# Loading weight tiles in pairs: one 2 MB transfer and one signal for two tiles

## What is computed

```
def reference(x, mem, ...):
    x = first_block(x, mem, ...)
    return second_block(x, c_2, ...)

first_block:
    proj = rmsnorm(h) @ w_in                    # conv, q, k, v, q_mem and gate columns
    y_conv = conv_module(u_conv, ...) @ w_conv_out
    y_attn = chunk_attention(q, k, v, rel_bias) @ w_attn_out
    kv = rmsnorm(mem) @ w_mem_kv
    y_mem = memory_attention(qm, km, vm) @ w_mem_out
    h = h + (g0 * y_conv + g1 * y_attn + g2 * y_mem) @ w_o
    val, gt = split(causal_dwconv(rmsnorm(h) @ w_up))
    h = h + (silu(gt) * val) @ w_down
second_block:
    mod = silu(c) @ ada_w + ada_b               # six vectors of 2048
    x = x + g1 * token_mixer(h, w_in, ...)      # four kinds of attention
    x = x + g2 * moe_ffn(h, ...)                # 16 experts, each token uses two of one group of four
```

## Time and profile before

| | us |
|---|---|
| median of 3 runs | 3329.46 |
| their range | 3325.71 to 3338.23 |
| the profiled execution | 3333.14 |
| its span in the profile | 3331.4 |
| PE busy | 3166.1 (95%) |
| DVE busy | 2060.5 (62%) |
| ACT busy | 1420.9 (43%) |
| DMA, mean of the span | 208 GB/s |

### The profile page before, as it was taken

One profiled execution on the slowest core, in us unless ns is written; L12 is line 12 of the kernel. 1 busy time (PEld: TensorE's weight loads), 2 busy tenths in 40 slices (PEclk: granted clock), 3 DMA queues, 4 the chain that ended last, 5 costly groups with the idle time before them and its releaser, 6 DMA issues.

```text
span 3331.4 us, 54295 instructions
## 1 busy us (share of the span) xinstructions
PE 3166.1 (95%) x21868; PEld 2979.2 (89%) x21868; DVE 2060.5 (62%) x2409; ACT 1420.9 (43%) x1531; POOL 69.7 (2%) x171
## 2 busy tenths in 40 slices
PE   6899999998998999999999799999897999999997
PEld 6789699998998999999999799977696988989887
DVE  4434347887664889889888533124453586685774
ACT  4433353434434444444444332123332465475562
POOL 0000100000000000000000000002100000000000
PEclk8999699999998999999999898575596999999999
DMA  6335245553553788788887664222230688596782
GB/s 222 139 132 184 91 169 188 178 187 139 205 190 118 301 332 320 307 327 315 322 321 287 182 209 151 76 60 50 65 114 7 250 337 316 217 381 228 303 325 88
DMA packets 114005, 694.25 MB, mean 208 GB/s; under 512 B 13984, under 2 KB 27536, under 8 KB 32464
## 3 DMA queue, kind: packets, MB, share of 16 engines
q1 hardware_dynamic: 107648, 671.14, 53.8%
q10 hardware_dynamic: 4688, 13.11, 1.4%
q0 software_dynamic: 1536, 8.13, 0.9%
HBM read 681.83 MB, written 10.49 MB: 208 GB/s over the span
## 4 chain that ended last, share of the span: by engine, by line
PE 90%; DVE 5%; DMA 2%; ACT 1%; issue 1%; SPq 0%; DVEq 0%; ACTq 0%
PE psT L847 17%; PE psT L848 17%; PE psT L849 17%; PE psT L1198 2%; PE psT L1200 2%; PE psT L1199 2%; PE psY L968 2%; PE psT L1187 2%; PE psT L1189 2%; PE psT L1188 2%; PE psY L940 2%; PE psT L892 1%; PE psY L1005 1%; PE psT L893 1%; PE psT L894 1%; PE psY L1088 1%
## 5 line engine op out<-in xcount | busy, mean ns | idle before, releaser
L1312 DVE TENSOR_TENSOR w_lo<-raw,w_hi 128x2048 fp32r<-128x2048 f32 x532 | 1217.1, 2291 | 693.0 <-ACT w_hi L491 689.9
L491 ACT ACTIVATE w_hi<-raw 128x2048 fp32r<-128x2048 f32 x532 | 1016.7, 1912 | 661.1 <-PE psT L849 204.2
L847 PE MATMUL psT<-a_hi,w_hi 128*128 128x256 f32 x4304 | 1227.1, 285 | 53.2 <-DVE a_lo L1339 48.0
L848 PE MATMUL psT<-a_lo,w_hi 128*128 128x256 f32 x4304 | 1224.8, 285 | 0.0
L849 PE MATMUL psT<-a_hi,w_lo 128*128 128x256 f32 x4304 | 1224.5, 284 | 0.0
L847 PEld LDWEIGHTS psT<-a_hi,w_hi 128*128 128x128 f32 x4304 | 833.7, 194 | 55.6 <-issue 50.6
L848 PEld LDWEIGHTS psT<-a_lo,w_hi 128*128 128x128 f32 x4304 | 833.7, 194 | 0.1
L849 PEld LDWEIGHTS psT<-a_hi,w_lo 128*128 128x128 f32 x4304 | 833.4, 194 | 0.0
L1525 DVE CUSTOM_DVE_ANT_0 pool<-pool 128x2048 f32<-128x2048 f32 x96 | 219.3, 2284 | 0.0
L847 PE MATMUL psT<-h_hi,w_hi 128*128 128x256 f32 x704 | 200.7, 285 | 5.8 <-DVE h_lo L1557 5.7
L848 PE MATMUL psT<-h_lo,w_hi 128*128 128x256 f32 x704 | 200.4, 285 | 0.0
(11 more groups left out here) (275 smaller groups left out, 3868.3 us busy)
## 6 DMA issues: line engine op xcount, KB each, us to landing
raw<-tiles_dram SPq DMA_DIRECT2D x532, 1024.0 KB, 5.3
pool<-ada_tiles_dram SPq DMA_DIRECT2D x96, 1024.0 KB, 4.8
bias_rows_dram<-pool ACTq DMA_DIRECT2D x1, 8192.0 KB, 50.4
pool<-bias_rows_dram SPq DMA_DIRECT2D x40, 128.0 KB, 2.2
pool<-w_dram POOLq DMA_DIRECT2D x8, 512.0 KB, 6.3
pool<-bias_rows_dram SPq DMA_DIRECT2D x40, 64.0 KB, 1.8
pool<-mem_dram ACTq DMA_DIRECT2D x1, 2048.0 KB, 13.5
pool<-x_dram ACTq DMA_DIRECT2D x1, 2048.0 KB, 23.8
```

Source lines behind the costliest of these rows:

```text
L491: nc.scalar.activation(w_hi[:, t.k % SPL, :], raw[:, t.k % RAW, :], ACT.Copy).then_inc(hi_done, 1)
L847: nc.tensor.matmul(ps_out, wh, x_hi, start=first, stop=False)
L848: nc.tensor.matmul(ps_out, wh, x_lo, start=False, stop=False)
L1312: nc.vector.tensor_tensor(w_lo[:, t.k % SPL, :], raw[:, t.k % RAW, :], w_hi[:, t.k % SPL, :].bitcast(F32), ALU.subtract).then_inc(lo_done, 1)
```

## The change

Two tiles are loaded by one DMA into two neighbouring places of the ring, and there are two semaphores, one for each pair of places. `load_tile` does nothing for an odd tile. For an even tile t it waits for `lo_done` of tile t - 3, so that both places are free, and issues one transfer of 2 MB. The destination names 128 partitions, 2 tiles, 2048 elements. `load_expert` does the same in steps of two. `split` waits for the pair's semaphore, for either tile of the pair. The ring's size, the order on ACT, DVE and PE, and the ada loads are as before.

```diff
-        landed = [sem(f"tile_landed{s}") for s in range(RAW)]
+        landed = [sem(f"tiles_landed{s}") for s in range(RAW // 2)]
...
             def load_tile(t):
-                wait(sp, lo_done, (t + -RAW).count())
-                sp.dma_start(raw[:, t.k % RAW, :], tiles[t.k if t.i is None else t.i * t.n + t.k])\
-                    .then_inc(landed[t.k % RAW], 16)
+
+                if t.k % 2:
+                    return
+                wait(sp, lo_done, (t + (1 - RAW)).count())
+                at = t.k if t.i is None else t.i * t.n + t.k
+                sp.dma_start(raw[:, t.k % RAW:t.k % RAW + 2, :], tiles[bass.ds(at, 2)].rearrange("t p n -> p t n"))\
+                    .then_inc(landed[t.k % RAW // 2], 16)
...
-                for k in range(4):
+                for k in (0, 2):
                     t = Tile(at + k)
-                    wait(sp, lo_done, (t + -RAW).count())
-                    sp.dma_start(raw[:, t.k % RAW, :], tiles[group[s] * 48 + (BASE["moe"] + 12 * j + 4 * part + k)])\
-                        .then_inc(landed[t.k % RAW], 16)
+                    wait(sp, lo_done, (t + (1 - RAW)).count())
+                    first = group[s] * 48 + (BASE["moe"] + 12 * j + 4 * part + k)
+                    sp.dma_start(raw[:, t.k % RAW:t.k % RAW + 2, :], tiles[bass.ds(first, 2)].rearrange("t p n -> p t n"))\
+                        .then_inc(landed[t.k % RAW // 2], 16)
...
-                act.wait_ge(landed[t.k % RAW], t.plus(16 * (t.k // RAW + 1), 16 * (t.n // RAW)))
+                act.wait_ge(landed[t.k % RAW // 2], t.plus(16 * (t.k // RAW + 1), 16 * (t.n // RAW)))
```

## The result

| us | before | after |
|---|---|---|
| median of 4 runs | 3328.57 | 3448.98 |
| their range | 3325.71 to 3338.23 | 3444.68 to 3459.76 |
| the profiled execution | 3333.14 | 3447.05 |
| its span | 3331.4 | 3445.3 |

The changed kernel takes 1.0361 times as long (95% interval 1.0329 to 1.0394): 3.6% slower, 17 us more than the 3432 us forecast and inside its range.

What follows compares the result with a forecast made beforehand. TensorE was taken to bound the kernel, with loads hidden. Kernel start 2, feed-forward 24, experts' start 2.4 and window runs 74 added 102.4 us to 3333.1, giving a median of 3432 us (3.1% slower), range 3392 to 3480.

Steps and rivals of the forecast that it cites:

- The trip of a ring place: All stages: load, w_hi, w_lo, next load must fit four tiles of PE, 23.0 us, or 10.9 in window runs.
- Plain stages: Attention weights, gates, projections: the later landing, 8.2 us in all for an even tile, stays hidden; cost 0.
- Window runs: Three runs of 40 window-expert tiles: rounds of 14.0 us against PE's 10.9 lose 67 us, 74 with spacing.
- the 7 us added for spacing: Window runs: loaded tiles stand 2.75 us apart, not 2.48; half of up to 4.9 us a run was added.
- Feed-forward: Feed-forward stage: 22 us of drift less 2 for w_lo's lead over PE, plus 4 at the start: 24 us.
- The drift: Feed-forward: DVE's chain takes 71.3 us per 12 tiles against PE's 69.1, so 2.2 us too slow, ten groups.
- Start of the experts: Tile 340, which nothing hides, now lands with tile 341, 2.48 us later: cost 2.4 us.
- Kernel start: First tiles: the third tile lands with the fourth, so its w_lo ends at 32.2 instead of 30.2: cost 2 us.
- Rival 1: Whole kernel: lateness is hidden, same or slightly faster, 3322 us; needs 2 MB landing in under 4.2 us; chance 0.05.
- Rival 3: Window runs and feed-forward: a 2 MB load costs 0.5 us more than two of 1 MB, 3461 us; chance 0.15.
- Rival 2: Window runs: the clock also falls to 1.2 GHz in each of 27 rounds, 46 us more, 3480 us; chance 0.10.
- Granted clock 1.00 in the runs: Window runs: a sign expected in the profile after, the granted clock staying at its full value of 1.00.

Runs made afterwards that it cites:

- Plain pairs: Pair first's kernel with pairs kept only for tiles 0 to 339 and expert tiles loaded one by one: 3327.5 us, ratio to before 0.9958 to 1.0046.
- quads: Changed kernel taken one step further, four tiles in one 4 MB transfer into the whole ring with one signal: 4510.3 us in one run.
- Pair first: Changed kernel with each feed-forward pair load put ahead of the ada load it stood behind on SP: 3410.9 us.
- own signals: Changed kernel with pairs still issued together, but each tile having its own transfer and semaphore: 3357.4 us, ratio to before 1.0065 to 1.0138.
- late signal: Kernel before, with single loads issued as early, but w_hi of an even tile also waiting for the odd one: 3492.0 us.
- the two runs on shape: Changed kernel with each pair as two 1 MB transfers on one semaphore, 3442.4 us; or contiguous as 16 KB per partition, 3451.6 us.

## Why the prediction was right

**The method.** The trip of a ring place, compared with what PE needs for four tiles, named the two stages that lose and the ones that don't. Plain stages differ by -4.0 and -0.4 us. Plain pairs and quads show both sides of that limit. Of the 17 us between forecast and median, 11.5 lie in the stages. The other 5.6 lie between executions: the profiled execution before is now 4.6 us above its median (3.7 when the forecast was made), the one after 1.9 below. And the 11.5 are small partly by luck, since the clock took 4 us off in the plain stages.

**Window runs, 74 forecast, 86 measured.** The step held and its terms were small by little. With the 7 us added for spacing the forecast stood at 14.27 us a round; measured is 14.42. Landing took 7.5 us, not 7.3. The rounds make only 4 of the 12 us missing: nine of them, from the end of w_lo of tile 359 to that of tile 395 and so in the other two runs, took 128.8, 130.4 and 130.2 us against 128.4. Another 6 lie behind them, where the forecast had put nothing. PE starts on the last tile of a run 0.7, 0.7 and 2.0 us after its w_lo, and in two runs it then needs 1.7 and 1.3 us more for the next tile, whose w_lo ends 1.3 and 1.0 us after PE is done with the last. Some 1 us more comes from following the first run alone: in the kernel before, PE reached the last tile 103.8 us after the first w_lo there, but 103.1 in the other two. The Trainium skill (SBUF — State Buffer, The DMA setup-cost knee) would give 6.8 us for 2 MB, an estimate by its formula; measured is 7.5 to 7.6. For 4 MB the same estimate is 11.6, measured 12.3.

**Feed-forward, 24 forecast, 28 measured.** The drift was forecast at 2.2 us in 12 tiles. From tile 187 to 271, PE's distance to before at every twelfth tile is 5.4, 7.6, 9.9, 12.1, 14.1, 16.2, 18.4 and 20.6 us: 2.2 each. Its cause was the one named: rows of SP and DVE after the change, for tiles 202 and 203, the pair ahead of that of the earlier trace rows; the last row of SP is the pair twelve tiles on.

```profile
1354.81 0.33 SPq L429 DMA_DIRECT2D pool<-ada_tiles_dram  x1
1355.34 0.39 SPq L383 DMA_DIRECT2D raw<-tiles_dram  x1
...
1426.72 0.39 SPq L383 DMA_DIRECT2D raw<-tiles_dram  x1
```
```profile
1352.34 2.29 DVE L1530 CUSTOM_DVE_ANT_0 pool<-pool 128x2048 f32<-128x2048 f32 x1
...
1366.71 2.29 DVE L1317 TENSOR_TENSOR w_lo<-raw,w_hi 128x2048 fp32r<-128x2048 f32 x1 [0.29 <-ACT w_hi L496]
```

From the dot product's end (1354.63) to w_lo of the even tile (1366.71) are 12.1 us, as worked out. Tile 214, at the same place of the next twelve, is issued 71.4 us later (1355.34 to 1426.72), where 71.3 was worked out and PE needs 69.1. Pair first shows that it was this link. What was off were the ends. The start (tiles 152 to 167) cost 7.8 us where 4 was put and the last four tiles 2.6 us. The drift between them, to tile 279, came to 17.6 us, that of eight groups of twelve and not ten; I had put 22 and deducted 2 for the lead of w_lo.

**Start of the experts, 2.4 forecast, 3.9 measured.** I priced the pair's landing by the second of two single loads. SP and ACT after the change:

```profile
2603.20 0.96 SPq L473 DMA_DIRECT2D raw<-tiles_dram  x2
```
```profile
2610.90 3.71 ACT L496 ACTIVATE w_hi<-raw 128x2048 fp32r<-128x2048 f32 x2 [13.18 <-DMA raw<-tiles_dram]
```

From issue to w_hi are 7.70 us, where one tile takes 4.8: 2.9 more, not 2.5. With own signals the start loses 0.6 us, with a late signal 3.7, so it is the joint signal that costs here; the last microsecond is not explained further.

**Kernel start, 2 forecast, 1.0 measured.** Of no weight; the range of runs is wider.

**Rival 1** (hidden) is out: pairs land in 7.5 us, far over 4.2. **Rival 3** (2 MB costs more) is out at its size by the two runs on shape. **Rival 2** (the clock falls) happened and did not cost what it was given. Rounds of the window runs of the changed kernel, from one end of w_lo to the next; the first two at full clock, the others where it fell:

```profile
2722.61:2736.85 14.24, 13.47 (x61) 11.15 (x62) 10.42 (x7) 7.75 (x7) 0.00 (x0) 1.00 0.83 296
2823.03:2837.18 14.15, 13.12 (x58) 10.56 (x57) 8.98 (x5) 7.44 (x4) 0.00 (x0) 1.00 0.82 296
2808.49:2823.03 14.54, 13.77 (x53) 11.35 (x54) 10.35 (x7) 8.47 (x6) 0.00 (x0) 0.80 0.78 288
3009.68:3025.27 15.59, 14.82 (x57) 12.19 (x58) 10.34 (x7) 8.94 (x7) 0.00 (x0) 0.81 0.74 270
3253.99:3269.48 15.49, 14.73 (x61) 12.26 (x61) 10.43 (x7) 9.08 (x7) 0.00 (x0) 0.89 0.74 272
```

"Granted clock 1.00 in the runs" was wrong: over the first run it was 0.95, with stretches of 3.4 to 6.8 us at the level of 1.2 GHz after PE had paused. But of 24 rounds 22 last 14.0 to 14.7 us, at 1.00 and at 0.79 alike. Two last some 1.1 us longer, both with a fall. PE's slower work goes mostly into the time it would have waited. If the fall is what made these two rounds longer, it cost 2.3 us there, and in the third run, where PE took the last tile at a mean clock of 0.74, 1.6 us more: at most some 4 us, not 46. The Trainium skill (TensorE: Matmul & The Clock Gate, HAM oscillation — how this bites in real kernels) describes groups of matmuls that are shorter than the DMA wait behind each, and are throttled again every time. Here PE was busy for 98 of the 115 us from 2722.61 to 2837.18, and the clock fell three times in these eight rounds; the rule as the prediction took it, a fall in each round, did not hold.

## What to carry to other kernels

A ring of four places loaded in pairs is a ring of two: the release comes one tile later and the signal one tile later, and both fall into the same round trip. Work that trip out for each stage and compare it with what the consumer needs for the whole ring. Where it has room, pairs cost next to nothing and gain nothing; where it has none, each microsecond of lateness is paid in every round, and two small delays cost more together than one by one (86 us against 24 and some 30).

If the fixed cost of transfers is to be saved, keep a signal for each tile: issuing together cost 1.0%, issuing and signalling together 3.6%. And look at what stands between two loads in their queue: one ada load there, released by the same engine that waits for the tiles, was worth 90 us with a joint signal.

## What the runs showed of the hardware

**The clock in the attention stage.** PE's time from tile 323 to 339 was 286.1 us in the profiled executions of before and after, and 270.1 to 270.6 in those of late signal, pair first and plain pairs. Pair first differs from the changed kernel in the feed-forward alone, so the edit isn't the cause. Same stage, before and then pair first: the whole of it, then 48 us in its middle.

```profile
2226.43:2512.51 286.08, 272.76 (x1305) 218.88 (x1304) 128.72 (x500) 104.57 (x281) 38.75 (x98) 0.67 0.24 72
2321.43:2369.43 48.00, 48.00 (x147) 33.22 (x146) 20.34 (x148) 17.41 (x65) 11.04 (x30) 0.50 0.17 38
```
```profile
2226.82:2496.89 270.07, 251.84 (x1305) 205.29 (x1304) 128.53 (x500) 104.66 (x281) 38.75 (x98) 0.75 0.26 76
2321.82:2369.82 48.00, 46.11 (x168) 31.82 (x166) 23.14 (x168) 19.52 (x73) 12.03 (x33) 0.64 0.18 41
```

The instructions are the same in number; the granted clock returns to full some 50 us earlier in the one. What decides it stayed open. Executions of one kernel scatter too: thirteen of the kernel before took 3292.2 to 3336.9 us, the two fastest at a mean clock of 0.937 to 0.939 and most others at 0.92; that this stage makes the difference there isn't shown. It is a reason to compare stages rather than totals where 16 us matter.

**Landing.** From the medians of issue to signal, in stretches without ada loads: 1 MB 4.8 us, 2 MB 7.5 to 7.7, 4 MB 12.3. Beyond the first, each MB adds 2.3 to 2.9 us. At 2 MB it makes 0.2 us whether a partition's 16 KB are contiguous or not (7.7 and 7.5).
